# One addition of eight token-sum units moved from GpSimd to VectorE, and engine queues written in another order, in a hybrid convolution and mLSTM layer

## The reference

```python
xn = rmsnorm(x, norm_gain)
proj = jnp.einsum('btd,dp->btp', xn, w_in)
gb, gc, hc, zc, q, k, v, o, zm, ig, fg = jnp.split(proj, ...)
yc, conv_new = short_conv(gc * hc, conv_buf, conv_w)      # 3 taps
y_conv = gb * yc * jax.nn.silu(zc)
# mLSTM in chunks of 128 tokens, 4 heads of 128, state (c, n, m)
s = jnp.einsum('bhjd,bhsd->bhjs', q, k) * d
num = jnp.einsum('bhjs,bhsv->bhjv', s, v) + inter[..., None] * jnp.einsum('bhjd,bhdv->bhjv', q, c_prev)
h = num / jnp.maximum(jnp.abs(den), jnp.exp(-m_t))[..., None]
c_new = decay[..., None, None] * c_prev + jnp.einsum('bhs,bhsd,bhsv->bhdv', w_last, k, v)
h = rmsnorm_per_head(h) * mh_norm_gain
y_m = (h * jax.nn.sigmoid(o)) * jax.nn.silu(zm)
out = jnp.einsum('btw,wd->btd', jnp.concatenate([y_conv, y_m], axis=-1), w_out)
y = rmsnorm(x + out, final_norm_gain)
```

## Time and profile before

| | us |
|---|---|
| median of three runs | 1123.94 |
| the runs | 1123.94, 1123.08, 1523.97 |
| the profiled execution | 1122.66 |
| its span in the trace | 1120.8 |
| TensorE busy | 1026.9 |
| VectorE busy | 658.8 |
| ScalarE busy | 420.7 |
| GpSimd busy | 430.5 |

### The profile page before, as it was taken

The page is one execution under the profiler, slowest core; times in us unless marked ns, Lnnn a source line. Parts: engine busy times, 40 slices in busy tenths (PEclk is TensorE's granted clock), DMA queues, the critical chain, the costliest instruction groups (busy, mean ns, idle before and its releaser), DMA issues.

```text
span 1120.8 us, 22712 instructions
## 1 busy us (share of the span) xinstructions
PE 1026.9 (92%) x9052; PEld 775.8 (69%) x9052; DVE 658.8 (59%) x1156; ACT 420.7 (38%) x868; POOL 430.5 (38%) x477
## 2 busy tenths in 40 slices
PE   1998889899789798999899999999999999999996
PEld 1754546455378687999888899979889999544442
DVE  5785765565667675555675555567655454433333
ACT  5644352523343343334533343435243333211111
POOL 5211324546553583523542342417042331442422
PEclk9998999999899999999999999999999999999998
DMA  9485551725660356491605362925152749355651
GB/s 242 142 173 130 156 148 37 217 61 178 213 217 21 100 163 211 133 343 58 220 25 176 101 207 87 324 74 190 39 187 82 258 91 382 137 199 207 233 213 79
DMA packets 192077, 180.86 MB, mean 161 GB/s; under 512 B 44600, under 2 KB 152260, under 8 KB 191972
## 3 DMA queue, kind: packets, MB, share of 16 engines
q1 hardware_dynamic: 160880, 142.76, 40.7%
q0 software_dynamic: 7600, 25.03, 6.1%
q10 hardware_dynamic: 23492, 11.63, 3.6%
HBM read 120.48 MB, written 50.19 MB: 152 GB/s over the span
## 4 chain that ended last, share of the span: by engine, by line
PE 61%; DVE 19%; POOL 5%; ACT 5%; DMA 4%; issue 3%; SPq 2%; DVEq 0%; ACTq 0%; POOLq 0%
PE bank L1329 11%; PE bank L1331 10%; PE bank L1330 10%; PE bank L1555 4%; PE bank L1554 4%; PE bank L1553 4%; DVE yc L205 2%; DVE gatebuf L205 2%; DVE Wl L205 2%; DVE xs L205 2%; DVE u L205 2%; PE bank L1486 2%; PE bank L1487 2%; PE bank L1485 2%; PE bank L1130 1%
## 5 line engine op out<-in xcount | busy, mean ns | idle before, releaser
L1329 PE MATMUL bank<-xTh,Wh 128*128 128x256 f16 x768 | 212.0, 276 | 17.3 <-ACT bank L205 9.8
L1330 PE MATMUL bank<-xTl,Wh 128*128 128x256 f16 x768 | 211.6, 276 | 0.0
L1331 PE MATMUL bank<-xTh,Wl 128*128 128x256 f16 x768 | 211.5, 275 | 0.0
L1130 PE MATMUL bank<-xTh,Wh 128*128 128x512 f16 (+2 forms) x440 | 122.5, 312 | 8.3 <-DVE Wl L205 7.8
L1131 PE MATMUL bank<-xTl,Wh 128*128 128x512 f16 (+2 forms) x440 | 122.8, 311 | 0.0
L1132 PE MATMUL bank<-xTh,Wl 128*128 128x512 f16 (+2 forms) x440 | 122.7, 311 | 0.0
L1329 PEld LDWEIGHTS bank<-xTh,Wh 128*128 128x128 f16 x768 | 76.0, 99 | 29.9 <-ACT bank L205 10.4
L1329 PE MATMUL bank<-xTh,xs 128*128 128x256 f16 x288 | 79.2, 275 | 10.5 <-DVE xs L205 10.5
L1330 PEld LDWEIGHTS bank<-xTl,Wh 128*128 128x128 f16 x768 | 76.1, 99 | 11.0 <-issue 0.7
L1331 PEld LDWEIGHTS bank<-xTh,Wl 128*128 128x128 f16 x768 | 76.0, 99 | 9.6
L1331 PE MATMUL bank<-xTh,xs 128*128 128x256 f16 x288 | 79.3, 275 | 0.0
(11 more groups left out here) (527 smaller groups left out, 2850.8 us busy)
## 6 DMA issues: line engine op xcount, KB each, us to landing
xTh<-x_ops SPq DMA_DIRECT2D x12, 1280.0 KB, 9.4
xTl<-x_ops SPq DMA_DIRECT2D x12, 1280.0 KB, 12.7
wst<-in_w_in SPq DMA_DIRECT2D x25, 512.0 KB, 5.1
xs<-in_x_prompt SPq DMA_DIRECT2D x22, 512.0 KB, 4.2
y_ops<-ysumst POOLq DMA_DIRECT2D x16, 512.0 KB, 3.3
xTh<-x_ops SPq DMA_DIRECT2D x12, 512.0 KB, 5.1
xTl<-x_ops SPq DMA_DIRECT2D x12, 512.0 KB, 5.8
out<-xs POOLq DMA_DIRECT2D x11, 512.0 KB, 2.9
```

What stands on the lines that cost most here:

```text
L1130: mm(out, wh[:, k, :], xh, start=(k == 0), stop=False)
L1329: mm(out, wh[:, k, :], xh, start=(first and k == 0), stop=False, skip_group_check=not first)
L1330: mm(out, wh[:, k, :], xl, start=False, stop=False, skip_group_check=not first)
L1331: last = mm(out, wl[:, k, :], xh, start=False, stop=(k == KT // 2 - 1), skip_group_check=not first)
```

## The change

- **Normalisation of a unit.** The gain multiplies x by norm_gain alone and waits for the squares' read of x only; ScalarE's high part takes rsx as its scale and VectorE's low part multiplies by rsx as it subtracts.
- **Prologue.** The first weight is split before units 2 to 4 have their high and low parts, on both engines. SyncE turns units 5 and 6 and loads units 8 and 9 ahead of three loads of weights.
- **Units one tile earlier.** Each entry of X_SQUARE and X_PARTS stands about one tile earlier, and the gain of a unit stands behind the low part of the unit before.
- **Token sums of the first head.** VectorE makes the first of the five (`token_sums_first`, placed by S_FIRST), GpSimd the other four. The units are taken and stored earlier, six of them (S_FLAT) through the flat buffers, and GpSimd's block order is written anew.
- **Raw weights of the second head.** GC and HC are loaded without a wait, K, Q and V wait for six stored units.
- **Splits in block 3.** Split 2 stands at GB instead of HC, splits 5 and 6 at O instead of ZM.
- **Stream.** Split 16 follows split 15; low split 13 follows the second half of u; the last convolution tap follows seed 2; the fifth product's evacuation precedes the exponentials; splits 5 and 6 for the next head come earlier; the high and low parts of token sums 8 and 13 move from the end of a block into the next one; GpSimd's token sums 8 stand ahead of a store.

```diff
-X_SQUARE = [{Q: 6, GC: 7, HC: 8, ZC: 9, O: 10}, {K: 11, V: 12, GC: 13, HC: 14}, {K: 15, V: 16}]
-X_PARTS = [{Q: 5, GC: 6, HC: 7, GB: 8, O: 9, ZM: 10}, {V: 11, Q: 12, HC: 13, GB: 14}, {V: 15, Q: 16}]
+X_SQUARE = [{V: 6, Q: 7, GC: 8, HC: 9, ZC: 10, O: 11}, {K: 12, V: 13, Q: 14, HC: 15}, {K: 16}]
+X_PARTS = [{V: 5, Q: 6, GC: 7, HC: 8, ZC: 9, O: 10}, {K: 11, V: 12, Q: 13, HC: 14}, {K: 15, V: 16}]
...
-S_TAKE = [{}, {ZM: 0}, {K: 1, HC: 2, ZM: 3}, {K: 4, Q: 5, HC: 6, GB: 7}]
-S_STORE = [{}, {}, {K: 0, V: 1, GB: 2}, {K: 3, V: 4, GC: 5, GB: 6, ZC: 7}]
+S_TAKE = [{}, {ZC: 0, ZM: 1}, {V: 2, HC: 3, ZM: 4}, {K: 5, Q: 6, HC: 7}]
+S_LOW = [{}, {ZC: 0, ZM: 1}, {V: 2, HC: 3, ZM: 4}, {K: 5, Q: 6, GB: 7}]
+S_STORE = [{}, {O: 0}, {K: 1, Q: 2, GB: 3}, {K: 4, V: 5, GC: 6, ZC: 7}]
+S_FLAT = 6
+S_FIRST = [{}, {HC: 0, ZC: 1, ZM: 2}, {GC: 3, ZC: 4, ZM: 5}, {K: 6, GC: 7}]
...
@@ SyncE
             load_x(7)
+            turn_x(5)
+            load_x(8)
             next_w(6)
             next_w(7)
-            turn_x(5)
-            load_x(8)
+            turn_x(6)
+            load_x(9)
             next_w(8)
...
                 if u == S_HEAD:
-                    sp.wait_ge(op_low, splits(1, SPLITS - 1))
+                    sp.wait_ge(op_low, splits(1, T_SPLIT[2] + 1))
...
-            sp.wait_ge(s_out[0], 32 * 2)
-            sp.wait_ge(s_out[1], 32 * 2)
-            for t in (K, Q, V, GC, HC):
+            load_raw(1, GC)
+            load_raw(1, HC)
+            for i in range(2):
+                sp.wait_ge(s_out[i], 16 * S_FLAT)
+            for t in (K, Q, V):
                 load_raw(1, t)
...
@@ GpSimd, token_sums
-                if u < S_HEAD:
-                    x, y = (t[:, :, tok0(b):tok0(b) + BT].rearrange("p (h k) t -> p h k t", h=2)[:, :, k, :] for t in (xTh, xTl))
-                    ins = pool.tensor_tensor(f, x, y, ALU.add)
-                else:
+                if u == S_HEAD:
+                    pool.wait_ge(op_low, splits(1, SPLITS - 1))
+                if u >= S_HEAD:
+                    pool.wait_ge(s_low, u - 1)
                     pool.wait_ge(unit_in, 16 * (u - S_HEAD + 1))
...
                 pool.wait_ge(s_sums, 5 * u + 1)
...
@@ GpSimd, pool_block
-                if b == NB - 1:
-                    token_sums(5)
                 if b:
+                    if first:
+                        x_power((12, 16)[b - 1])
+                    if b == NB - 1:
+                        token_sums(6)
                     store_y(g, b - 1, 1)
...
+                    if b == 2:
+                        token_sums(3)
...
                 if b == 1:
...
+                    token_sums(0)
                 if b == NB - 1:
-                    token_sums(6)
                     token_sums(7)
+                    weight_sums(1, 0)
                 store_y(g, b, 0)
-                if b == NB - 1:
-                    weight_sums(1, 0)
                 if b in (1, 2):
-                    token_sums((0, 3)[b - 1])
...
+                    token_sums((1, 4)[b - 1])
...
                 if b in (1, 2):
-                    token_sums((1, 4)[b - 1])
+                    token_sums((2, 5)[b - 1])
...
@@ GpSimd, pool_stream_block
+                    if B == 0:
+                        token_sums(8)
                     store_mixed(g, 0)
...
@@ ScalarE
+                act.wait_ge(x_rs, unit + 1)
                 act.wait_ge(x_gained, unit + 1)
-                mark(fn(x_high_rows(unit)[0:n, :], x_raw[i][0:n, :], ACT.Copy).then_inc(x_high, 1), x_high, unit + 1)
+                mark(fn(x_high_rows(unit)[0:n, :], x_raw[i][0:n, :], ACT.Copy, scale=rsx[0:n, unit:unit + 1]).then_inc(x_high, 1), x_high, unit + 1)
...
                 fifth(g, b, 0)
+                if B in (1, 2):
+                    token_sums_high((8, 13)[B - 1])
...
                 seed(g, b, 1)
+                fifth(g, b, 1)
...
                 exps(n, eh, A, 4, a_free, n * 3 + 1)
-                fifth(g, b, 1)
...
                 if late:
                     split_high(late, 15)
+                    split_high(late, 16)
...
                 seed(g, b, 3)
-                if late:
-                    split_high(late, 16)
...
                 mark(fn(first_half(to), XB, ACT.Tanh, scale=0.5 / WS).then_inc(x_free, 1), x_free, m[3] + 1)
+                if prep:
+                    split_high(prep, 5)
...
                 if prep:
-                    split_high(prep, 5)
+                    split_high(prep, 6)
...
                 head_squares(n, (0, 1))
-                if prep:
-                    split_high(prep, 6)
-                if B == 0:
-                    token_sums_high(8)
-                if B == 1:
-                    token_sums_high(13)
...
-                        for i in {GC: (0, 1), HC: (2,), ZC: (3, 4), ZM: (5, 6)}.get(t, ()):
+                        for i in {GC: (0, 1), GB: (2,), ZC: (3, 4), O: (5, 6)}.get(t, ()):
...
             x_square(2)
+            load_w(act, 0, 1)
             x_square(3)
-            load_w(act, 0, 1)
-            x_square(4)
+            split_w(0, 0)
             x_high_part(2)
             load_w(act, 0, 2)
+            x_square(4)
...
-            split_w(0, 0)
             x_high_part(4)
...
@@ VectorE
-                dve.wait_ge(x_rs, unit + 1)
-                mark(stt(x[0:n, :], x[0:n, :], rsx[0:n, unit:unit + 1], fgain[0:n, :], ALU.mult, ALU.mult).then_inc(x_gained, 1), x_gained, unit + 1)
+                dve.wait_ge(x_sq, unit + 1)
+                mark(tt(x[0:n, :], x[0:n, :], fgain[0:n, :], ALU.mult).then_inc(x_gained, 1), x_gained, unit + 1)
...
-                mark(tt(x_low_rows(unit)[0:n, :], x[0:n, :], x_high_rows(unit)[0:n, :], ALU.subtract)
+                mark(stt(x_low_rows(unit)[0:n, :], x[0:n, :], rsx[0:n, unit:unit + 1], x_high_rows(unit)[0:n, :], ALU.mult, ALU.subtract)
...
+            def token_sums_first(u):
...
+                if u == S_FLAT + 1:
+                    dve.wait_ge(t1_free, t1(0, NB - 2, "next cols", True) + 1)
+                if u < S_HEAD and k == 0:
+                    for unit in x_units(b):
+                        x_turned(dve, unit)
+                f = s_stage(u)[0].rearrange("p (h t) -> p h t", h=2)
+                x, y = (t[:, :, tok0(b):tok0(b) + BT].rearrange("p (h k) t -> p h k t", h=2)[:, :, k, :] for t in (xTh, xTl))
+                if u:
+                    dve.wait_ge(s_sums, 5 * u)
+                mark(tt(f, x, y, ALU.add).then_inc(s_sums, 1), s_sums, 5 * u + 1)
...
                 heads_out(g, b, s_t0(n, "hT"), A)
+                if B in (1, 2):
+                    token_sums_low((8, 13)[B - 1])
...
-                did(stt(yc[:, :], u[:, 2:2 + BT], cwt[:, bass.ds(g, 1), 2], yc[:, :], ALU.mult, ALU.add))
...
                 seed(g, b, 2)
+                did(stt(yc[:, :], u[:, 2:2 + BT], cwt[:, bass.ds(g, 1), 2], yc[:, :], ALU.mult, ALU.add))
...
                 if late:
                     split_low(late, 15)
+                    split_low(late, 16)
...
                 second_of_second(g, b, 3, ctmp, False)
+                if prep:
+                    split_low(prep, 5)
...
                 head_norms(n)
+                if prep:
+                    split_low(prep, 6)
...
-                if B == 0:
-                    token_sums_low(8)
-                if B == 1:
-                    token_sums_low(13)
-                if prep:
-                    split_low(prep, 5)
-                    split_low(prep, 6)
...
-                    if first and t in X_PARTS[b]:
-                        x_gain(X_PARTS[b][t])
+                    if first and b == 0 and t == V:
+                        x_gain(X_EARLY)
...
                             x_low_part(X_PARTS[b][t])
+                        if t in X_SQUARE[b]:
+                            x_gain(X_SQUARE[b][t])
                     at_end(g, b, t, first)
-                    if t in S_TAKE[b]:
-                        token_sums_low(S_TAKE[b][t])
+                    if t in S_LOW[b]:
+                        token_sums_low(S_LOW[b][t])
+                    if t in S_FIRST[b]:
+                        token_sums_first(S_FIRST[b][t])
...
-                        if t == HC:
+                        if t == GB:
                             split_low(1, 2)
...
-                        if t == ZM:
+                        if t == O:
                             split_low(1, 5)
                             split_low(1, 6)
...
             x_gain(3)
+            split_w(0, 0)
             x_low_part(2)
             x_gain(4)
             x_low_part(3)
-            split_w(0, 0)
```

61 lines of the change are left out of this document (24 added, 37 removed).

## The result

| | before | after |
|---|---|---|
| median, us | 1124.43 | 1106.39 |
| runs shown, us | 1123.08 to 1523.97 | 1104.85 to 1107.82 |
| span of the profiled execution, us | 1120.8 | 1105.8 |

The ratio is 0.9852, with a 95% interval of 0.9836 to 0.9868: by the ratio 16.6 us faster, under half of the 40 that were forecast. The time is inside the range of 1064 to 1108, at its upper end, and outside the range that the forecast gave itself (1064 to 1099). The gain is clear of the noise, but it lies within the 2% to which the prediction gave a chance of 0.15. One run of before, at 1523.97, was disturbed: it is not in the ratio, but it is in the median of 1124.43 (1123.94 without it).

The account below looks back on a forecast made before the run. TensorE, busy 1026.9 of 1120.8 us, was taken as the bound, its gaps ended by late VectorE or ScalarE entries. First head 17.7 plus stream 21.8 gave 39.5: 1122.7 - 39.5 = 1083.2, as a median 1084; range 1064 to 1108.

Parts of the forecast that it names:

- the sum of the first head, 17.7: First head: gains 1 + 8.6 + 4.9 + 7.1 + 2, less 4.9 for sums and 1 for columns, give 17.7 us.
- Start, 1: Prologue: the first weight's low part comes some 7 us earlier, but TensorE then waits for turned units; 1 us, ends 0 and 4.
- Gates, 8.6: Gates of block 1 and the next: waits for turned units of 6.1 us go, with 2.5 of clock; 8.6, lower end 4.3.
- sel, 4.9: Block 2: unit 16's gain goes a tile earlier; 3.1 of the 4.0 us wait and 1.8 of clock; ends 1.9 and 5.8.
- Update, 7.1: Block 3: unit 7's low part no longer late; the 7.3 us gap falls to 2, with 1.8 of clock; ends 5 and 9.1.
- Into the stream, 2: Start of the stream: low split 5 moves ahead, leaving ScalarE's seed next late; 2 us gained, ends -1 and 4.4.
- The sums' price, 4.9: First head: eight first sums on VectorE at 1.23 us, half in front of TensorE; 4.9 us lost, ends 0 and 16.8.
- The stream, 21.8: Streamed heads: moved high parts, splits, fifth product and conv tap close waits; 5.8 + 6.0 + 5 + 4 + 2 + 1.5 - 2.5 = 21.8 us.
- Rival 4: Block 3: unit 7's chain is no shorter, so 7.1 falls to 2; 1089 us, inside the forecast's 0.68.
- Rival 2: Streamed heads: moved entries only trade waits; the stream gives 4 us, the first head 15; 1105 (1098 to 1115), chance 0.12.
- Rival 1: First head: VectorE's queue replaces GpSimd's, all eight sums at 2.10 in front, 16.8 us; 1096 (1088 to 1108), chance 0.17.
- Rival 3: Block 3: contention stretches VectorE's work 2.4 times, making the kernel slower; 1170 us, chance 0.03.

Follow-up runs that it names:

- sp_order: stream_only with SyncE storing the tokens of blocks 0 and 1 behind the turns of units 8 and 12; 1102.6 us, 0.981.
- sp_low7: sp_order with unit 7's low part moved from ahead of the update to behind the reciprocal, its high part and store a little later; 1099.2 us, 0.978.
- sums_pool: The changed kernel with the first token sum of all eight units given back to GpSimd; 1106.5 us, 0.9854.
- sums_none: The changed kernel with VectorE's first sum of units 0 to 6 cut to 16 of 1024 columns; 1100.6 us, 0.9796.
- stream_only: The kernel before with the change's edits of the streamed heads alone; 1108.7 us, 0.9881.
- first_alone: The kernel before with only the first token sum of units 0 to 7 moved from GpSimd to VectorE; 1125.5 us, 1.002.
- pool_light: The changed kernel with GpSimd's token sums of the first head and the second head's first weight sums cut to one column; 1090.8 us, 0.9706.
- behind: The changed kernel with VectorE's normalisation steps of a unit set behind the first half of the next tile's work; 1114.9 us, 0.9917.
- block3: The changed kernel with unit 7's low part, low splits 2 and 6 and GpSimd's first weight sums moved in block 3; 1106.6 us, 0.9847.
- order3: sp_low7 with gain 16 behind sel, split 2 a tile later and split 5 a tile earlier; 1099.1 us, 0.978.
- order4: sp_low7 with split 2 behind the late update, splits 5 and 6 a tile earlier, unit 7's low part and store behind them; 1098.6 us, 0.978.

## Why the prediction was wrong

**The step that failed is the sum of the first head, 17.7.** It took each closed gap as time kept: gates 8.6 + sel 4.9 + update 7.1 + stream 2. The lead shows 0.9 at its end: the listed waits fell by 1.8 us only, and the half clock cost 2.9 more. In the steps below it is -1.3 + 7.65 - 6.05 + 1.4 - 3.5 + 3.6 - 0.9.

- *Start, 1:* the weight's low part did come 6.9 us earlier, and TensorE then waited for turned units, as said; but the lead fell to -1.3, below the lower end 0. ScalarE's high part of unit 5, now in tile V, waits for VectorE's gain behind the gate chain, with the evacuation of V and the small qfm queued behind it: the 3.7 us wait for qfm, and 6.8 us at 1.2 GHz where before had 3.4. This was a moved entry that added a wait, and I had not costed ScalarE's side of it.
- *Gates, 8.6:* right for the long wait, -0.7 to 6.35 is 7.1 of 4.4 + 2.5. Of the 1.7 in the next gates only some 0.5 went: TensorE waits 1.3 there for cs. sp_order got about the same, 8 (0.9881 to 0.981), by SyncE's order alone.
- *Between 98 and 172 us, 1 for the columns:* 6.05 were lost (6.35 to 0.3). The waits there grew from 8.4 to 11.2 us in all: ysum 2.8 for 2.0, cs 2.5 for 2.1, a new 1.0 for tom, and 3.6 for 1.9 at a cn that stands behind first sum 0 and a gate chain stretched beside GpSimd's sums (its scan 1.63 for 1.22). Three half-clock stretches cost 5.1 where one cost 1.7. This span has no other term in the sum.
- *sel, 4.9:* the wait fell from 4.0 to 2.4, the clock fell as before: 1.4 (0.3 to 1.7). sel no longer stands behind the gain of unit 16, but behind the low part of token unit 2 (200.29, 1.23 us), which the new tables put there.
- *Between 203 and 278 us, no term but the sums' price:* 3.5 lost (1.7 to -1.8), by waits of 0.6, 1.3 and 1.4 for cn, dp and u that before doesn't have. dp ran at 258.09 right behind first sum 6 (256.73, 1.23 us), and the first sum of unit 7 (273.36, 2.31 us) stands ahead of u.
- *Update, 7.1:* the wait fell from 7.3 to 4.0, the stretch at 1.2 GHz from 6.8 to 3.4 us; 3.6 of lead (-1.8 to 1.8), below the end of 5. I put 5.3 of the wait down to unit 7's late low part, and it was 3.2 (sp_low7). That part did go, because the unit is taken earlier and not because of the engine: in sums_pool the update waits 4.1. The rest is VectorE's own queue, nearly twice as slow beside GpSimd.
- *Into the stream, 2:* split 5 came earlier, and the lead rose to 5.2; but splits 5 and 6 ran at 2.12 and 2.10 beside GpSimd's weight sums in front of the evacuation that the seed waits for, and the longest stretch at 1.2 GHz, 10.2 us, followed: 1.8 to 0.9 over all, just inside the ends.
- *The sums' price, 4.9:* near right. sums_none gives 6.3 for seven. Seven of the eight ran at 1.23; the one of unit 7 took 2.31. What failed is what they were to buy: on GpSimd the same sum cost no more (sums_pool).
- *Two readings* were wrong too. The half clock's cost was put at 13.1 from seven stretches; the trace has nine, and it was 16.5. And the gaps were not all ended by VectorE's or ScalarE's queue: the 6.1 for xTl hung on SyncE's.

**The stream, 21.8:** the mechanism was right and the sizes were off: 14.5 in the lead, 13.4 in stream_only. The Wl, xs and dpm rows are gone as forecast. The two seeds' gaps of 4.9 closed to 2.2 and less, not to nothing: 4.3 and 4.9 of lead for 5.8 and 6.0. No token sum stands ahead of these seeds any more; what is left of the first stands behind the den step, which took 2.66 us (2.41 before). The price of 2.5 was too low: TensorE waits 4.9 for VectorE's seeds where it waited 2.8 (I had that fall by 1.5), and the two waits of 1.5 and 1.4 that appear behind the first moved high part, at 395 and 400 us, are new.

**The rivals.** Rival 4 (the move itself does nothing) is what happened, with the reason that it gave (first_alone), but I had it cost 5.1 of 39.5, as if the other terms stood by themselves. Rival 2's time, 1105, is right for the wrong reason: it had the stream trade waits and the first head keep 15, and it was the other way round. Rival 1 took VectorE's queue as the limit, which holds, but by dearer sums, which were mostly not dear. Rival 3 did not come; VectorE's stretching existed before the change too.

**The signs** that I had named: no gate wait for xTl over 1 us, right; cn under 3 us, wrong (8.2); no ScalarE seed held by a token sum, right; xs under 4, right; VectorE busier by about 10 in the first head, wrong (178.3 to 182.6 us, up to the stream under way); GpSimd less by 17 to 20, a little short (104.5 to 88.7); fewer half-clock stretches, 7 for 9, right. Of the signs against, one first sum of eight took over 2 us, the waits for ysum and for one cn in block 1 grew to 2.8 and 3.6, and the first head was as long as before (318.0 us until the stream is under way).

**What stays open.** sums_none and pool_light leave work out, so they say what holds the first head, not how to do it in the same time. Leaving the sums out also makes their results ready sooner; how much of the 16 us is that and how much VectorE's stretch is shown for the update of block 3 alone. GpSimd's sums were left out of the changed kernel only, not of sp_low7. That any order closes the last waits isn't excluded: four were tried (behind, block3, order3, order4) and moved them.

## What to carry to other kernels

A gap that closes early in a stretch is worth only what no later entry takes back: follow the lead of the same instruction through both traces, and cost the end of the stretch and not the gaps one by one. Before an elementwise step is moved between two engines, try the move alone and leave the step out once: here the step stood in the path on either engine. When reordering only moves the waits on, compare the duration of the queue's entries with their shortest in the same trace; if they are stretched, it is the neighbour's load that has to go, and a late entry that hangs on a queue of transfers, like unit 8's turn behind a store, is the one that order does cure.

## What the hardware showed that I had not expected

VectorE is slowed by GpSimd's sums in entries of many kinds with no operand in TensorE's banks, even a one-operand tap (from 0.49 to 1.48 us) and an entry of two columns (par, from 0.17 to 1.11), and not in those that take an operand from a bank: u<-bank,gcs takes 0.69 in both. Counted over the whole trace of the changed kernel, 127 entries with an operand from a bank ran for more than half of their time beside a sum of GpSimd, and none took over 3% more than the shortest of its kind; the 142 without one took 1.56 times the shortest of theirs together. The Trainium skill, page GPSIMD Engine Reference, section Specifications, names contention with VectorE instructions that have two SBUF inputs or run in a 2-port perf mode; both traces agree with it as to two inputs, and the rows above (10.4 against 5.7 us for the same entries) are its size here. In which mode the entries of one operand ran, no run here shows.

In all, GpSimd's sums cost TensorE 16 us in the changed kernel, about half by waits and half by the clock, in a head in which GpSimd is busy for 88.7 of 269 us and not once named in TensorE's waits.
